# Ten blocks of expert rows instead of eleven, a seventh weight buffer, and a later start for the gathers of stored results

## The chip, the cores and the metric

The kernel runs on one core of one Trainium2 chip. The metric is the device time of one launch in microseconds (us). Three runs of the kernel before gave 803.15, 804.07 and 806.66 us, so the median is 804.07 us.

A core has a matrix engine (TensorE, PE in the profile), a vector engine (DVE), a scalar engine (ACT), GpSimd (POOL) and a sync engine (SP) that here only issues transfers. Sixteen DMA engines serve all queues. PE writes its products to eight banks of PSUM; everything else lies in SBUF or in device memory.

## The reference: what is computed

A trunk of two layers over 384 tokens (128 context, 256 latent) of width 1024, in float32. Each layer has a mixer (attention and a state-space scan behind one input projection, one output projection) and then a mixture of experts. The change concerns the mixture alone:

```python
def moe_ffn(h, w_router, router_bias, w_gate_l, w_up_l, w_down_l):
    ...
    best = jnp.argmax(grp_score, axis=-1)
    masked = jnp.where(in_group, sel, NEG_INF)
    _, idx = lax.top_k(masked, TOP_K)          # TOP_K = 2 of 16 experts
    ...
    hid = jax.nn.silu(einsum('nd,edf->enf', t, w_gate_l)) * einsum('nd,edf->enf', t, w_up_l)
    hid = hid * gates.T[:, :, None]
    out = jnp.einsum('enf,efd->nd', hid, w_down_l)
```

An expert has a gate and an up matrix (1024 x 256) and a down matrix (256 x 1024), 1 MiB each. So a layer reads 48 MiB of expert weights. The 384 tokens make 768 choices. The number of tokens that the reference sends to each expert can be counted from the given inputs. In layer 0, experts 0 to 15 get 38, 35, 30, 51, 43, 30, 42, 31, 99, 72, 105, 52, 45, 13, 45 and 37 tokens. In layer 1 they get 57, 50, 46, 37, 21, 24, 31, 26, 48, 76, 62, 38, 69, 49, 47 and 87.

## The kernel before, in words

**Blocks.** The kernel computes rows of tokens in blocks of 128. The shapes are fixed when the program is built, while the counts are known only when it runs. So each expert has a capacity in rows. In the kernel before, experts 0 and 1 are fixed and have 128 rows each. The other 14 are ranked by their counts at run time: the four most loaded have 128 rows each, the ten others 64. A block holds one expert of 128 rows or two of 64, which makes eleven blocks (`BLOCKS`, `PAIRS`).

**Overflow.** If an expert gets more tokens than its capacity, the rest is computed in extra rounds. DVE takes the largest excess over the capacities (`combination`) and derives `rounds`; each engine then reads that number and, if it is over zero, runs `overflow`: per round a loop over all 16 experts, one after the other (`again` on each engine). Of each expert it makes the list of tokens, gathers 128 rows, loads the three matrices (3 MiB), multiplies, and stores 128 rows. SP loads an expert's matrices only once the expert before it has been multiplied, since one pair of buffers serves all. After the 16 experts, six gathers and six pairs of DVE operations add the results to `x`, one after the other (`gather_results`, `add_results`).

**A block on the engines.** POOL gathers the block's rows from `h_rows` by an indirect DMA. PE transposes them (L2202), multiplies with gate and up (`gate_up`, L2212), transposes the hidden rows (L2219) and multiplies with down (`down`, L2228). DVE and ACT carry the data between these (L1556, L984, L1561, L1567, L991). Eight blocks are stored by ACT to `y_exp` in device memory. The last three (`LATE`) stay in SBUF, and PE adds them by products with a selection matrix (L2272). The order on PE is fixed in the code: while block b waits for its hidden rows, the gate-up product of block b+1 runs.

**Where an expert's rows stand in the array.** A block with one expert is multiplied as 128 columns of the array; one with two experts as two tiles of 64 columns, an instruction for each (`n = P // len(slots)`).

**Weights.** SP loads weights into a ring of `SLOTS` = 6 buffers of 2 MiB. A unit is either the gate and up of one expert or the down matrices of a pair. `MOE_UNITS` gives the order, `EARLIER` the unit whose use frees the buffer. The units of ranked experts can be issued only when DVE has written `order` (L1436, semaphore `s_order`). PE waits for a unit by `landed`.

**The end of a layer.** When all blocks but the last three are stored, POOL issues six gathers from `y_exp` (L714), two for each of three groups of 128 tokens. ACT and DVE weight and add them (L1001, L1544), DVE multiplies with the gate (L1549, L1550), then adds the late blocks (L1656). SP loads the next layer's input projection only when the last of these gathers has landed.

Of the kernel before, what the change touches and what calls it, by code (L numbers as in the profile page):

```python
# [12 lines left out]
P = 128  # L13
DM = 1024
KT = DM // P
# [18 lines left out]
FIXED = 2  # L34
# [6 lines left out]
SLOTS = 6  # L41
# [12 lines left out]
for _l in range(DEPTH):  # L54
# [6 lines left out]
    assert len(ORDER) % SLOTS == 0  # L61
# [3 lines left out]
PAIRS = ("fixed", "light", "heavy", "light", "heavy", "light", "light", "light")  # L65
BLOCKS = [(_p, _part) for _p, _kind in enumerate(PAIRS)
          for _part in (((0, 1),) if _kind == "light" else ((0,), (1,)))]
NB = len(BLOCKS)
HEAVY = 2 * PAIRS.count("heavy")
_heavy, _light = iter(range(HEAVY)), iter(range(HEAVY, RANKED))  # L70
RANK_AT = [None if _kind == "fixed" else tuple(next(_heavy if _kind == "heavy" else _light) for _ in range(2))
           for _kind in PAIRS]
GU_BLOCK = [[b for b, (p, part) in enumerate(BLOCKS) if p == pp and k in part][0]
            for pp in range(len(PAIRS)) for k in range(2)]
# [5 lines left out]
LATE_RANKS = [r for p, part in BLOCKS[STORED:] for r in (RANK_AT[p][k] for k in part)]  # L80
assert all(len(part) == 2 for p, part in BLOCKS[STORED:]) and LATE_RANKS == list(range(RANKED - 2 * LATE, RANKED))
stores_of = lambda i: len(range(i, STORED, 2))
DN_BLOCK = [max(b for b, (p, _part) in enumerate(BLOCKS) if p == pp) for pp in range(len(PAIRS))]
MOE_UNITS = []
for _b in range(NB + 1):
    for _p, _ks in ([(BLOCKS[_b][0], BLOCKS[_b][1])] if _b < NB else []) + ([(BLOCKS[_b - 1][0], (2,))] if _b else []):
        MOE_UNITS += [(_p, _k) for _k in _ks if (_p, _k) not in MOE_UNITS]
# [4 lines left out]
def product_order():  # L92

    last = []
    for l in range(DEPTH):
        before = range(MOE_AT[l - 1] + MOE_U if l else 0, MOE_AT[l])
        last += sorted(before, key=lambda u: (u >= IN_AT[l][1], u == IN_AT[l][0], u))
        for b in range(NB + 1):
            if b < NB:
                last += [MOE_AT[l] + UNIT_AT[BLOCKS[b][0], k] for k in BLOCKS[b][1]]  # L100
            if b and DN_BLOCK[BLOCKS[b - 1][0]] == b - 1:
                last += [MOE_AT[l] + UNIT_AT[BLOCKS[b - 1][0], 2]]
    return last
# [4 lines left out]
SLOT, EARLIER = [], []  # L108
for _u in range(len(ORDER)):
    if _u < SLOTS:  # L110
        SLOT.append(_u)
        EARLIER.append(None)
        continue
    _holder = {s: max(v for v in range(_u) if SLOT[v] == s) for s in range(SLOTS)}
    _s = min(_holder, key=lambda s: RELEASED[_holder[s]])
# [10 lines left out]
def hybrid_step(nc, x_prompt, x_sample, cache_k, cache_v, state_ssm, c, c_ctx, norm1_w, norm2_w,  # L126
# [9 lines left out]
    with ctx:  # L136
# [9 lines left out]
        xn = sb("xn", NT, DM)  # L146
# [5 lines left out]
        xpad = sb("xpad", XM * 512)  # L152
# [136 lines left out]
        y_exp = nc.dram_tensor("y_exp", [STORED * CAP, DM], fp32)  # L289
# [6 lines left out]
        landed = [sem(f"landed{i}") for i in range(SLOTS)]  # L296
        s_rows, s_x, s_small, s_state = sem("rows_landed"), sem("x_landed"), sem("small_landed"), sem("state_landed")
        s_snw, s_fnw = sem("snw_landed"), sem("fnw_landed")
# [58 lines left out]

        def gate_up_of(s):

            return ring[:, s, :].rearrange("p (i k f) -> p k i f", i=2, k=KT)  # L360
# [43 lines left out]
        LISTS = ((0, 1), (1, 2), (2, 7), (7, NB))  # L404
        ROWS_AT = 5
# [36 lines left out]
        def _(sp):  # L442
# [19 lines left out]
            def columns(u, w):  # L462
# [3 lines left out]
                load(u % SLOTS, [(slot(u)[:, 4 * i:4 * i + 4, :], v[:, 4 * i:4 * i + 4, :]) for i in range(2)])  # L466
# [13 lines left out]
            def expert_unit(l, pair, j, u):  # L480

                s = SLOT[u]
                if j < 2:
                    load(u % SLOTS, [(ring[:, s, i * KT * F:(i + 1) * KT * F], by_row(w[l, pair[j]]))
                             for i, w in enumerate((w_gate, w_up))])
                else:
# [1880 lines left out]
```

## Time and profile before

| | us |
|---|---|
| median of 3 runs | 804.07 |
| the profiled execution | 801.22 |
| its span, first to last instruction | 799.5 |
| PE busy | 743.1 (93%) |
| DVE busy | 328.9 (41%) |
| ACT busy | 216.1 (27%) |
| POOL busy | 142.9 (18%) |
| DMA, mean rate | 265 GB/s, 211.56 MB |

All rows that are shown are from the one profiled execution, whose own time is 1.6 us over its span. It is 2.9 us under the median of the three runs. PE is busy nearly all the time, but a busy PE says little by itself: the profile must be read stage by stage. The mixture of experts of layer 0 runs from about 255 to 414 us, that of layer 1 from about 631 to the end.

### The profile page before, as it was taken

Reading aid. Unit: us, or ns where it says so; the run is one execution under the profiler, and the core shown is the slowest. Engines: PE = TensorE matmul, PEld = TensorE weight load, DVE = VectorE, ACT = ScalarE, POOL = GpSimd, SP = SyncE. Lnnn points to the kernel's source line nnn. Section 1 sums busy time; section 2 is a strip of 40 time slices with the busy share of each in tenths; the row PEclk is TensorE's granted clock in tenths of the full one; section 3 lists DMA queues with packets and bytes.
Section 4 is the critical chain, followed back from the end, with each engine's and each line's share of the span. In section 5 each row is a group of like instructions: output and inputs, shape, how many; then the busy total and the mean of one; then the engine's idle time right before and its main releaser. Section 6 shows DMA issues by size and latency. Waiting matters only on the chain. (4 is left out here: it accounts for less than half of the span.)

```text
span 799.5 us, 9607 instructions
## 1 busy us (share of the span) xinstructions
PE 743.1 (93%) x3542; PEld 374.4 (47%) x3542; DVE 328.9 (41%) x870; ACT 216.1 (27%) x491; POOL 142.9 (18%) x238
## 2 busy tenths in 40 slices
PE   3999998999998999999899999888999899999994
PEld 1456653545446444443344755344544654444331
DVE  2023534735536453212272252564643744331136
ACT  2210255734023110111312025493411311101121
POOL 4146041120010200000112404122000120000102
PEclk9999999999999999999999999999999999999998
DMA  8997228899601999999897233345420399999961
GB/s 321 387 342 250 95 106 295 308 362 403 240 0 80 374 392 420 421 424 423 312 389 245 88 105 112 108 170 228 155 105 1 121 420 377 418 425 422 422 241 79
DMA packets 66340, 211.56 MB, mean 265 GB/s; under 512 B 7883, under 2 KB 8755, under 8 KB 54003
## 3 DMA queue, kind: packets, MB, share of 16 engines
q1 hardware_dynamic: 52744, 179.33, 57.9%
q10 hardware_dynamic: 7851, 17.70, 5.8%
q0 software_dynamic: 5696, 13.89, 4.8%
q8 instruction: 29, 0.48, 0.2%
q14 instruction: 20, 0.16, 0.1%
HBM read 202.02 MB, written 13.93 MB: 270 GB/s over the span
## 5 line engine op out<-in xcount | busy, mean ns | idle before, releaser
L2212 PE MATMUL bank<-ring,work 128*64 128x512 f32 (+1 forms) x512 | 156.5, 596 | 4.1 <-DMA ring<-in_w_up_dram 3.2
L2212 PEld LDWEIGHTS bank<-ring,work 128*64 128x64 f32 (+1 forms) x512 | 58.6, 157 | 96.2 <-issue 94.6
L2228 PE MATMUL bank<-ring,xs_tok 128*64 128x512 f32 (+1 forms) x256 | 79.9, 597 | 2.5 <-DVE xs_tok L1567 1.4
L1567 DVE COPY xs_tok<-bank 128x256 f32<-128x256 f32 x22 | 9.3, 425 | 150.7 <-PE bank L2219 150.7
L1850 PE MATMUL bank<-hT,ring 128*128 128x384 f32 x192 | 62.2, 486 | 0.0
L1724 PE MATMUL bank<-ring,cpad 128*32 128x512 f32 x384 | 48.6, 632 | 6.2 <-DMA ring<-in_w_ada_dram 5.4
L1850 PEld LDWEIGHTS bank<-hT,ring 128*128 128x128 f32 x192 | 36.5, 190 | 25.0
L2228 PEld LDWEIGHTS bank<-ring,xs_tok 128*64 128x64 f32 (+1 forms) x256 | 28.3, 157 | 39.6 <-issue 36.9
L984 ACT ACTIVATE xs_tok<-bank 128x256 f32<-128x256 f32 x22 | 8.5, 386 | 138.4 <-PE bank L2212 138.4
L2108 PE MATMUL bank<-ring,xn 128*128 128x512 f32 x96 | 43.6, 597 | 0.0
L991 ACT ACTIVATE qkv<-bank 128x512 f32<-128x512 f32 x40 | 21.7, 595 | 80.0 <-PE bank L2228 80.0
L2108 PE MATMUL bank<-ring,xs_tok 128*128 128x512 f32 x96 | 43.2, 592 | 0.0
L1795 PE MATMUL bank<-ring,hT 128*128 128x512 f32 x96 | 42.8, 597 | 0.4 <-ACT hT L797 0.4
L1907 PE MATMUL bank<-ring,hT 128*128 128x512 f32 x96 | 42.3, 593 | 0.0
L707 POOL DMA_INDIRECT hT<-h_rows,idx x18 | 18.4, 1024 | 124.0 <-PE bank L2202 77.1
L1556 DVE COPY work<-bank 128x512 f32<-128x512 f32 x42 | 27.1, 686 | 10.9 <-PE bank L2202 10.9
L1164 DVE SCALAR_TENSOR_TENSOR conv<-xpad,prm,conv 128x388 f32<-128x388 f32 x48 | 29.9, 623 | 1.7
L2108 PEld LDWEIGHTS bank<-ring,xs_tok 128*128 128x128 f32 x96 | 18.2, 190 | 23.0 <-issue 23.0
L1795 PEld LDWEIGHTS bank<-ring,hT 128*128 128x128 f32 x96 | 17.7, 190 | 22.6 <-issue 20.4
L1907 PEld LDWEIGHTS bank<-ring,hT 128*128 128x128 f32 x96 | 17.8, 190 | 20.1 <-issue 20.1
L2108 PEld LDWEIGHTS bank<-ring,xn 128*128 128x128 f32 x96 | 17.4, 190 | 19.2 <-issue 19.2
L1724 PEld LDWEIGHTS bank<-ring,cpad 128*32 128x32 f32 x384 | 10.8, 113 | 30.0 <-issue 21.7
(389 smaller groups left out, 1062.1 us busy)
## 6 DMA issues: line engine op xcount, KB each, us to landing
ring<-in_w_ada_dram SPq DMA_DIRECT2D x48, 1024.0 KB, 8.9
ring<-in_w_gate_dram SPq DMA_DIRECT2D x32, 1024.0 KB, 8.2
ring<-in_w_up_dram SPq DMA_DIRECT2D x32, 1024.0 KB, 12.3
ring<-in_w_down_dram SPq DMA_DIRECT2D x32, 1024.0 KB, 10.9
ring<-in_w_in_dram SPq DMA_DIRECT2D x16, 1024.0 KB, 14.4
ring<-in_w_out_dram SPq DMA_DIRECT2D x8, 1024.0 KB
y_exp<-qkv ACTq DMA_DIRECT2D x16, 512.0 KB, 8.1
xpad<-gate_rows ACTq DMA_DIRECT2D x6, 512.0 KB, 5.7
```

The costliest lines, as they stand in the source:

```text
L707: pool.indirect_dma_start(out=xg[b % 4], out_offset=None, in_=h_rows[:, :], in_offset=bass.IndirectOffsetOnAxis(ap=idx[:, b:b + 1], axis=0 ...
L991: act.activation(y_buf(e)[:, hf * 512:(hf + 1) * 512], bank[5 + hf][:, :], ACT.Copy).then_inc(s_yc, 1)
L1164: ins = dve.scalar_tensor_tensor(out=conv[:, m, :], in0=xpd[:, m, k:k + CONVW], scalar=tap(k), in1=conv[:, m, :], op0=ALU.mult, op1=ALU.add)
L1556: dve.tensor_copy(xgT[:, b, hf * 512:(hf + 1) * 512], bank[3 + hf][:, :]).then_inc(s_xgc, 1)
L1567: dve.tensor_copy(hidT[:, b, :], bank[2][:, 0:F]).then_inc(s_htc, 1)
L1724: last = mm(bank[ADA_BANK][ADA_TILE * q:ADA_TILE * (q + 1), :], cpad[:, c:c + ADA_TILE], slot(ADA_AT[j])[:, kt, :], start=j == a and kt < ...
L1795: last = mm(bank[t][:, :], tok(kt, t), slot(u[0])[:, kt, :], start=kt == 0, stop=kt == KT - 1)
L1850: last = mm(bank[(6 + m) % 8][:, 0:3 * P], slot(v)[:, kt, col:col + P], hT[:, kt, :], start=kt == 0, stop=kt == KT - 1)
L1907: last = mm(bank[4 + t][:, :], tok(kt, t), slot(u[3])[:, kt, :], start=kt == 0, stop=kt == KT - 1)
L2108: last = mm(bank[2 * t + hf][:, :], mixed[:, t, kt * P:(kt + 1) * P] if kt < 4 else xs_tok[:, t, (kt - 4) * P:(kt - 3) * P], slot(u + hf)[ ...
L2212: last = mm(bank[b][i * n:(i + 1) * n, :].rearrange("p (i f) -> p i f", i=2), rows_T[:, kt * P + i * n:kt * P + (i + 1) * n], gate_up_of(s ...
L2228: last = mm(bank[5 + hf][i * n:(i + 1) * n, :], hidT[:, b, f * P + i * n:f * P + (i + 1) * n], w[:, f, hf * 512:(hf + 1) * 512], start=f = ...
```

## The change

1. **Ten blocks.** Three experts are fixed, with 96 rows each. Of the 13 ranked ones the most loaded has 128 rows, the next three have 96, the other nine 64. The experts that have 96 rows share blocks with parts of 64 and 32 rows. Blocks 0, 2 and 4 hold parts of 64, 32 and 32 rows, one instruction for each; block 3 one of 128 rows; the others two of 64. Seven blocks are stored, three are late.
2. **A seventh buffer.** `extra` is a view of memory that held `xn` and `xpad`, now in one tensor, `arena`. It is free once the rows of `h` are stored, and used until block 5. A unit's semaphore is now one of seven (`LANDED`).
3. **Order of loads.** More is loaded before the ranking is known: experts 0, 1 and 2, and the down matrices of 0, 1 and 2. One unit is split for it (`SPLIT`).
4. **DVE's order.** The list of block 1 (now all fixed experts) is made behind `order`, and its row numbers behind another product.
5. **Gathers of results.** POOL waits for the last weight unit of the layer before it issues the six gathers. ACT and DVE weight them behind the last block.
6. **Capacities** in `combination` follow the new sizes; the overflow code is the same.

```diff
-FIXED = 2
+FIXED = 3
-SLOTS = 6
+SLOTS, EXTRA, LANDED = 6, 6, 7
...
+FULL, WIDE = 1, 4
+FIXED_CAP = 96
+cap_of = lambda r: CAP if r < FULL else HALF + CAP // 4 if r < WIDE else HALF
...
+Q = CAP // 4
+wide = lambda x: ((x, 0, HALF), (x, HALF, Q))
+BLOCKS = [parts_of(*wide(0), (1, 0, Q)),
+          parts_of((1, Q, HALF), (2, 0, HALF)),
+          parts_of(*wide(3), (2, HALF, Q)),
+          parts_of((4, 0, CAP)),
+          parts_of(*wide(5), (6, 0, Q)),
+          parts_of((6, Q, HALF), (7, 0, HALF))] + [parts_of((x, 0, HALF), (x + 1, 0, HALF)) for x in (8, 10, 12, 14)]
...
+SPLIT = (1, 2)
+MOE_UNITS = [(0, 0), (0, 1), (1, 0), (0, 2), SPLIT]
...
-        xn = sb("xn", NT, DM)
+        arena = sb("arena", NT * DM + XM * 512)
+        xn = arena[:, 0:NT * DM].rearrange("p (t c) -> p t c", t=NT)
...
+        xpad = arena[:, NT * DM:]
+        extra = arena[:, DM:DM + UNIT]
...
+                u = MOE_AT[l] + MOE_U - 1
+                pool.wait_ge(landed[u % LANDED], 32 * (u // LANDED + 1))
                 pool.wait_ge(s_yidx, l + 1)
...
                 for e in range(NB):
                     if e + 1 < NB:
                         silu(e + 1, (e + 1) % 2)
-                    if e == NB - 2:
-                        act.wait_ge(s_yidx, l + 1)
-                        weighted(0)
-                    if e == NB - 1:
-                        weighted(1)
-                        weighted(2)
...
                     store(e, e % 2)
+                act.wait_ge(s_yidx, l + 1)
+                for t in range(NT):
+                    weighted(t)
...
+                one_hots(*LISTS[1])
                 step(dve.tensor_tensor(by_rank, rt[:, 1, :, FIXED:E].unsqueeze(2).broadcast_to([P, NT, RANKED, RANKED]),
                                        perm.unsqueeze(1).broadcast_to([P, NT, RANKED, RANKED]), ALU.mult))
+                slot_tokens(1)
...
-                    dve.memset(cap_row[:, 0:FIXED], float(CAP))
+                    dve.memset(cap_row[:, 0:FIXED], float(FIXED_CAP))
...
-                    step(dve.tensor_scalar(cap_row[:, FIXED:E], rank, float(HEAVY), float(HALF), ALU.is_le, ALU.mult))
+                    dve.tensor_scalar(cap_stored[:, FIXED:E], rank, float(FULL), float(Q), ALU.is_le, ALU.mult)
+                    step(dve.tensor_scalar(cap_row[:, FIXED:E], rank, float(WIDE), float(Q), ALU.is_le, ALU.mult))
...
-                    step(dve.tensor_scalar(cap_row[:, FIXED:E], cap_row[:, FIXED:E], float(HALF), None, ALU.add))
+                    step(dve.scalar_tensor_tensor(out=cap_row[:, FIXED:E], in0=cap_row[:, FIXED:E], scalar=float(HALF),
+                                                  in1=cap_stored[:, FIXED:E], op0=ALU.add, op1=ALU.add))
...
                     step(dve.tensor_tensor(count, count, cap_row, ALU.subtract))
                     step(dve.tensor_reduce(top, count, AX.X, ALU.max))
...
-                        for i, s in enumerate(slots):
-                            last = mm(bank[b][i * n:(i + 1) * n, :].rearrange("p (i f) -> p i f", i=2),
-                                      rows_T[:, kt * P + i * n:kt * P + (i + 1) * n], gate_up_of(s)[:, kt, :, :],
+                        for s, at, n in parts:
+                            last = mm(bank[b][at:at + n, :].rearrange("p (i f) -> p i f", i=2),
+                                      rows_T[:, kt * P + at:kt * P + at + n], gate_up_of(s)[:, kt, :, :],
                                       start=kt == 0, stop=kt == KT - 1)
```

The first place is on PE, at the first block of a layer. Before, after the transposes of the rows, block 0 (one expert) is multiplied in instructions of 128 columns (the size is that of the output, columns by stream), four of gate-up ahead of the transposes of the next rows, and later the four of down:

```order
L2202 MATMUL bank<-ident,hT 128x128 x8
...
L2212 MATMUL bank<-ring,work 128x512 x4
L2202 MATMUL bank<-ident,hT 128x128 x8
...
L2219 MATMUL bank<-ident,xs_tok 128x128 x2
L2202 MATMUL bank<-ident,hT 128x128 x8
L2228 MATMUL bank<-ring,xs_tok 128x512 x4
```

Now block 0 alternates between an instruction of 64 columns and two of 32, eight times in gate-up and four times in down:

```order
L2279 MATMUL bank<-ident,hT 128x128 x8
...
L2288 MATMUL bank<-ring,work 64x512
L2288 MATMUL bank<-ring,work 32x512 x2
L2288 MATMUL bank<-ring,work 64x512
L2288 MATMUL bank<-ring,work 32x512 x2
...
L2303 MATMUL bank<-ring,xs_tok 64x512
L2303 MATMUL bank<-ring,xs_tok 32x512 x2
```

The tile size changes twice in each step of 128 input features, which happens nowhere in the kernel before.

On DVE, between the counts and the lists of the ranked blocks, the kernel before makes both fixed lists ahead of `order` (L1436); `idx` is what POOL's gathers wait for:

```order
L1418 TENSOR_TENSOR conv<-slots_f,qT 128x384 x2
...
L1406 SCALAR_TENSOR_TENSOR idx<-qT,bank 128x1
L1431 TENSOR_REDUCE qT<-qT 128x14
L1405 COPY qT<-bank 128x1
L1406 SCALAR_TENSOR_TENSOR idx<-qT,bank 128x1
...
L1436 TENSOR_SCALAR qT<-qT 128x14
L1438 TENSOR_TENSOR xs_tok<-qT 128x588
```

Now the second `idx`, that of block 1, stands behind `order` (L1523) and two more operations:

```order
L1485 SCALAR_TENSOR_TENSOR idx<-qT,bank 128x1
...
L1523 TENSOR_SCALAR qT<-qT 128x13
L1498 TENSOR_TENSOR conv<-slots_f,qT 128x3x64 x2
L1526 TENSOR_TENSOR xs_tok<-qT 128x507
L1484 COPY qT<-bank 128x1
L1485 SCALAR_TENSOR_TENSOR idx<-qT,bank 128x1
```

`order` moved ahead by the two operations of the second list and one of the first two lists, and block 1's row numbers moved behind it.

On SP, ahead of the first expert number that is read (`TENSOR_LOAD`), the kernel before loads two experts and two down matrices, and then three whole units:

```order
L460 DMA ring<-in_w_gate_dram 128x2048
L460 DMA ring<-in_w_up_dram 128x2048
L460 DMA ring<-in_w_down_dram 128x2048 x2
L510 TENSOR_LOAD qT
...
L460 DMA ring<-in_w_gate_dram 128x2048
L460 DMA ring<-in_w_up_dram 128x2048
```

Now three experts and three down matrices stand ahead of it; one unit and a half in the ring and one in `arena` follow:

```order
L527 DMA ring<-in_w_down_dram 128x2048 x3
L576 TENSOR_LOAD qT
...
L527 DMA ring<-in_w_gate_dram 128x2048
L527 DMA ring<-in_w_up_dram 128x2048
L527 DMA ring<-in_w_down_dram 128x2048
...
L527 DMA arena<-in_w_gate_dram 128x2048
L527 DMA arena<-in_w_up_dram 128x2048
```

Three MiB of the layer's 48 are thus asked for earlier than before, and 2 MiB more can be asked for while the ring is full.

## Rows read from the trace of the kernel before

**Rows 1.** Windows: us, busy PE PEld DVE ACT POOL, granted clock, DMA share, GB/s.
```profile
240.00:260.00 20.00, 17.64 (x146) 13.30 (x145) 13.04 (x45) 6.98 (x17) 1.99 (x3) 1.00 0.20 80
340.00:360.00 20.00, 20.00 (x74) 8.26 (x76) 3.66 (x7) 2.56 (x5) 0.00 (x0) 1.00 1.01 422
```
**Rows 2.** Timeline of PE, layer 0: start, us, what [idle before <-releaser].
```profile
268.22 1.04 PE L2202 MATMUL bank<-ident,hT 128*128 128x128 f32 x8
...
293.03 3.60 PE L2228 MATMUL bank<-ring,xs_tok 128*128 128x512 f32 x8
296.46 7.03 PE L2212 MATMUL bank<-ring,work 128*128 128x512 f32 x16
303.33 0.38 PE L2219 MATMUL bank<-ident,xs_tok 128*128 128x128 f32 x2
...
316.16 3.60 PE L2228 MATMUL bank<-ring,xs_tok 128*128 128x512 f32 x8
319.69 7.09 PE L2212 MATMUL bank<-ring,work 128*64 128x512 f32 x32
326.71 0.44 PE L2219 MATMUL bank<-ident,xs_tok 128*128 128x128 f32 x2
...
380.52 7.09 PE L2212 MATMUL bank<-ring,work 128*64 128x512 f32 x32 [1.81 <-DMA ring<-in_w_up_dram]
...
394.47 3.65 PE L2228 MATMUL bank<-ring,xs_tok 128*64 128x512 f32 x16 [1.09 <-DMA ring<-in_w_down_dram]
```
**Rows 3.** Timeline of SP, layer 0.
```profile
260.85 0.36 SPq L460 DMA_DIRECT2D ring<-in_w_gate_dram  x1
261.30 0.38 SPq L460 DMA_DIRECT2D ring<-in_w_up_dram  x1
...
396.48 12.70 SPq L460 DMA_DIRECT2D ring<-in_w_in_dram  x8
```
**Rows 4.** Timeline of POOL, layer 0.
```profile
258.70 1.18 POOL L707 DMA_INDIRECT hT<-h_rows,idx  x1 [12.77 <-DVE idx L1406]
260.19 1.05 POOL L707 DMA_INDIRECT hT<-h_rows,idx  x1 [0.30 <-issue]
...
383.68 0.99 POOL L714 DMA_INDIRECT xn<-y_exp,y_idx  x1 [0.31 <-issue]
```
**Rows 5.** Line L707 by itself: the gathers of rows, its last row.
```profile
DMA to landing us min/median/max: 9.0/10.1/11.7
```
**Rows 6.** Timeline, layer 0: first product of block 0's rows, end of the layer.
```profile
262.76 1.06 PE L2202 MATMUL bank<-ident,hT 128*128 128x128 f32 x8 [1.15 <-DMA hT<-h_rows,idx]
...
396.49 1.15 ACT L1001 ACTIVATE xn<-xn,wt 128x1024 f32<-128x1024 f32 x1 [0.38 <-DMA xn<-y_exp,y_idx]
397.73 1.28 DVE L1544 SCALAR_TENSOR_TENSOR xn<-xpad,wt,xn 128x1024 f32<-128x1024 f32 x1 [0.30 <-ACT xn L1001]
...
403.05 1.29 DVE L1656 TENSOR_TENSOR xn<-bank,xn 128x512 f32<-128x512 f32 x2 [1.52 <-PE bank L2272]
```
**Rows 7.** Timeline, end of layer 1.
```profile
774.26 1.15 ACT L1001 ACTIVATE xn<-xn,wt 128x1024 f32<-128x1024 f32 x1 [2.43 <-DMA xn<-y_exp,y_idx]
...
780.61 1.29 DVE L1656 TENSOR_TENSOR xn<-bank,xn 128x512 f32<-128x512 f32 x2 [1.30 <-issue]
```
**Rows 8.** Windows around a fall of the granted clock; columns as in the first group.
```profile
510.20:514.16 3.96, 1.90 (x10) 0.88 (x10) 3.00 (x12) 3.80 (x18) 2.46 (x4) 1.00 0.69 260
514.16:517.58 3.42, 3.42 (x20) 0.59 (x16) 1.04 (x4) 1.28 (x4) 0.03 (x1) 0.50 0.00 0
```
**Rows 9.** Timeline of PE: tiles of 32 columns, then of 64.
```profile
160.50 1.04 PE L1724 MATMUL bank<-ring,cpad 128*32 128x512 f32 x8
161.47 0.44 PE L1952 MATMUL bank<-qkv,ckv 128*64 128x256 f32 x2
```
**Rows 10.** Timeline, layer 0: hidden rows of a block with nothing beside them.
```profile
387.65 0.38 ACT L984 ACTIVATE xs_tok<-bank 128x256 f32<-128x256 f32 x1 [7.81 <-PE bank L2212]
388.36 0.41 DVE L1561 TENSOR_TENSOR xs_tok<-xs_tok,bank 128x256 f32<-128x256 f32 x1
388.50 3.65 PE L2228 MATMUL bank<-ring,xs_tok 128*64 128x512 f32 x16 [0.52 <-DVE xs_tok L1567]
```

More of the change, by code:

```diff
@@ L60, with parts_of @@
     MOE_AT.append(len(ORDER))
-    assert len(ORDER) % SLOTS == 0
     ORDER += [("moe", MOE_U * _l + j) for j in range(MOE_U)]
-PAIRS = ("fixed", "light", "heavy", "light", "heavy", "light", "light", "light")
-BLOCKS = [(_p, _part) for _p, _kind in enumerate(PAIRS)
-          for _part in (((0, 1),) if _kind == "light" else ((0,), (1,)))]
-NB = len(BLOCKS)
[L69 to L74, printed above, removed]
+FULL, WIDE = 1, 4
+FIXED_CAP = 96
+RANK_OF = [None if _x < FIXED else _r for _x, _r in zip(range(E), (0, 0, 0, 1, 0, *range(2, RANKED)))]
+assert sorted(_r for _r in RANK_OF if _r is not None) == list(range(RANKED))
+cap_of = lambda r: CAP if r < FULL else HALF + CAP // 4 if r < WIDE else HALF
+def parts_of(*parts):
+    at, out = 0, []
+    for x, lo, n in parts:
+        out.append((x, lo, n, at))
+        at += n
+    assert at == CAP
+    return tuple(out)
+Q = CAP // 4
[6 more added lines that the diff above has]
+          parts_of((6, Q, HALF), (7, 0, HALF))] + [parts_of((x, 0, HALF), (x + 1, 0, HALF)) for x in (8, 10, 12, 14)]
+NB = len(BLOCKS)
+experts_of = lambda b: list(dict.fromkeys(x for x, *_ in BLOCKS[b]))
+pairs_of = lambda b: list(dict.fromkeys(x // 2 for x in experts_of(b)))
+for _x in range(E):
+    _cap = FIXED_CAP if RANK_OF[_x] is None else cap_of(RANK_OF[_x])
+    _held = sorted((lo, n) for parts in BLOCKS for x, lo, n, _at in parts if x == _x)
+    assert sum(n for _lo, n in _held) == _cap and all(a + n == b for (a, n), (b, _n) in zip(_held, _held[1:]))
+GU_BLOCK = [max(b for b in range(NB) if x in experts_of(b)) for x in range(E)]
 BUFS, HOTS = 4, 5
@@ L108, with in_extra @@
 SLOT, EARLIER = [], []
+EXTRA_LAST = STORED
+def in_extra(u):
+    for at in MOE_AT:
+        if at + SLOTS <= u < at + MOE_U:
+            p, k = MOE_UNITS[u - at]
+            return (GU_BLOCK[2 * p + k] <= EXTRA_LAST) if k < 2 else DN_BLOCK[p] < EXTRA_LAST
+    return False
 for _u in range(len(ORDER)):
@@ L465, in columns @@
                     sp.wait_ge(*used(EARLIER[u]))
-                load(u % SLOTS, [(slot(u)[:, 4 * i:4 * i + 4, :], v[:, 4 * i:4 * i + 4, :]) for i in range(2)])
+                load(u % LANDED, [(slot(u)[:, 4 * i:4 * i + 4, :], v[:, 4 * i:4 * i + 4, :]) for i in range(2)])
             def ada_unit(u, n):
@@ L2193, in _ @@
                 lists(0)
+                clock_kept(2, 8)
                 lists(1)
[L2195 to L2198 removed]
                 def rows_transposed(buf, done):
@@ L2320, in again @@
                     pe.wait_ge(o_htc, q + 1)
-                    down(0, [ring[:, OVER_DN, 0:2 * DM]], o_dn)
+                    down(0, [(ring[:, OVER_DN, 0:2 * DM], 0, P)], o_dn)
                 def banks_read(steps):
```

206 lines of the change are left out of this document (114 added, 92 removed).

## The prediction

> **What bounds the kernel now.** I first read the windows of 20 us. Before 260 us the DMA engines move 80 GB/s; in the mixture of experts they move 422 GB/s with a busy share of 1.01, and PE is busy for all 20 of 20 us [rows 1]. So both are full there. Then I read PE's timeline. A block costs a down product and a gate-up product, each with small transposes: from the down at 293.03 to the next but one at 316.16, two blocks pass in 23.13 us, or 11.6 us each [rows 2]. PE waits only at the end, 1.81 us for one unit of weights and 1.09 us for the last [rows 2].
>
> How the DMA engines bound the stage follows from bytes. SP issues the first unit of a ranked expert at 260.85 and the next layer's weights at 396.48 [rows 3], 135.6 us later. Between lie 21 units of 2.10 MB and 25 transfers of rows of 0.52 MB (11 gathers of tokens, 8 stores, 6 gathers of results), 57.2 MB in all. That makes 422 GB/s, the rate of the window. The stage is thus bounded by DMA, with PE some 3 us less loaded. At the end DVE takes the last gathered result at 397.73 and reaches the late blocks at 403.05, having waited 1.52 us for PE [rows 4]. In layer 1 the gather is what the chain of waits goes through: ACT waits 2.43 us for it at 774.26 [rows 5].
>
> **The ten-block layout and its capacities.** The largest term is no term of the steady state. The new capacities of the ranked experts are 128 once, 96 three times, then 64. In layer 0 the ranked counts are 105, 99, 72, 52 and fewer: the second expert has 99 tokens and 96 rows. The largest excess is 3, `rounds` is 1, and every engine enters the overflow loop for all 16 experts. The kernel before had 128 rows for 99 tokens and no excess. In layer 1 the counts 87, 76, 69, 62, 49 fit, and so do the fixed experts in both layers (57 at most, of 96).
>
> The trace of before has no overflow, so the price of an expert is built from like operations. The count starts when PE has ended the down product of the expert before.
> - Weights: SP may issue only then. They are 3.15 MB. The gather of this expert's rows and the store of the last one's add 1.05 MB. At 422 GB/s [rows 1] that is 9.9 us; with some 2 us from the issue to the first data, 12 us.
> - Rows: the token list, its row numbers and POOL's issue take some 2 us. Under load a gather lands 9.0 us or more after its issue [rows 6]. Eight transposes (1.06 us, [rows 4]) and the copies (1.3 us) follow: 13.4 us. This ends later than the weights.
> - Gate-up at 128 columns: 6.87 us, from 296.46 to 303.33 [rows 2].
> - Hidden rows: gate-up of the last block ended at 380.52 + 6.87 = 387.39, its product on DVE at 388.77: 1.4 us; transposes and copy of the block before took until 388.50: 1.1 us [rows 2, 7]. Nothing hides these here: 2.5 us.
> - Down: 3.43 us, from 293.03 to 296.46 [rows 2].
> - Clock: after 4 us in which PE was busy for 1.90 us, the granted clock was 0.50, and it came back after 3.4 us in which PE was busy all the time [rows 8]. The two values are 1.2 and 2.4 GHz. In the loop PE is idle for some 12 of 27 us. I take 3.4 us of work at half speed per expert and the transposes at half too, +2.5 us.
> - Branch: reading the number of rounds and the branch cost DVE 1.30 us [rows 5]; of the loop's own branch I take 0.5 us.
>
> The sum is 13.4 + 6.9 + 2.5 + 3.4 + 2.5 + 0.5 = 29.2, and I take 29 us; 16 experts make 464 us. Its lower end is 24 us, if the gather hides behind the weights and the clock stays up (12 + 6.9 + 2.5 + 3.4, less a little overlap). Its upper end is 40 us, if all 12 us of PE's work run at half clock. That is 384 to 640 us for 16. Behind the loop stand six gathers in a row. Each takes 0.9 us from DVE to POOL and 4.1 us alone (258.70 to 262.76) [rows 4, 9]. Two operations of 1024 columns on DVE follow (1.28 us each) [rows 4], so one costs 7.9 us and six cost 47 us. With some 5 us for entering and for the row numbers, the round costs 464 + 52 = 516 us. Nothing hides it: the late results and the next layer need `x` behind it.
>
> **The rest of the change, by bytes.** After `order` there now are 19.5 units instead of 21 and 23 transfers of rows instead of 25: 53.0 MB, or 125.6 us at 422 GB/s. Three things take from these 10 us. The six gathers of results now run alone. They are issued 1.3 us apart, and one alone lands after 4.1 us: 10.6 us instead of 7.5 for the bytes, 3 us lost. Early in the stage the ring is still held by blocks 1 and 2: seven units are in or under way, and 5.2 MB last 12.4 us, while the next unit waits for gate-up of block 0, and the one of block 2 ends about 34 us after `order`. I estimate 5 us of idle DMA there, from 0 to 8. And block 1's row numbers now come behind `order`. POOL issued that gather at 260.19 [rows 9], ahead of SP's first load at 260.85 [rows 3], and PE took its rows at 268.22 without waiting [rows 2]. Now it is issued near 262, behind 3 MB of weights, and lands 9 us later, near 271: PE, and with it the ring, is some 3 us late (0.5 to 4), half of which the idle DMA above already has. What remains is about 2 us by which the last gather lands earlier. Layer 0 gains 1.5 us more, since DVE's wait for PE goes with the eleventh block, and layer 1 gets 2 us. That is -6 us in sum, from -16 (no idle DMA) to +2. The weighting behind the last block costs nothing: its gathers land later than that. The added operations of `combination` (some 0.2 us each) lie beside PE's second block, and the iotas of the start beside the first loads.
>
> A further term is open: blocks 0, 2 and 4 change between a tile of 64 columns and tiles of 32. Tiles of one size run side by side: 32 instructions of 64 columns take 7.02 us (319.69 to 326.71), 16 of 128 take 6.87 us [rows 2]. A change of size costs 0.10 us (316.16 to 319.69 is 3.53, where 293.03 to 296.46 without one is 3.43) and 0.15 us on the way back [rows 2]. From 32 to 64 columns it costs 0.11 us: eight instructions in two groups from 160.50 would let the next start at 161.36, and it started at 161.47 [rows 10]. In all these rows the tiles share columns. If the different sizes run side by side where they do not, the term is 0, which I take. If not, it is the second rival.
>
> On this the Trainium skill, TensorEngine Tiling (Array Packing), Key Properties, says that a change of tiling mode, not just of tile, drains the engine. By that rule the three blocks would be serial, and the sum would be that of the second rival; the rows above agree with a drain where tiles share columns, and none shows tiles that do not.
>
> **The sum.** 801.22 us, the profiled execution's own time, less 6 and plus 516 is 1311 us. The median lies 2.9 us above that execution: 804.07 + 510 = 1314 us.
>
> **Rivals.**
> 1. *The round runs, and the tile sizes do not run side by side.* A step of 128 input features takes 0.86 us now (6.87 / 8). It would take 0.86 for 64 columns, 0.86 for the two tiles of 32 and two changes of 0.25 us together: +1.11 us. Every instruction appears twice in the trace (16 issued, x32 shown). If the two halves alternate there are four changes, +1.36 us. A mixed block has 12 steps, so three blocks cost 40 to 49 us a layer. The block that is gone gives back 11.6, the waits for weights 3, and the later gather takes 3. PE then bounds the stage: +28 to +37 us a layer, 54 to 72 in sum, 60 to 78 over my forecast. That is 1383 us. For it: the change costs in each row where sizes differ. Against it: only shared columns were seen.
> 2. *The round does not run* (the other side). It is decided at one point: whether the second ranked expert of layer 0 has over 96 tokens on the chip. For it: no overflow ran in before, so nothing in the trace shows one. Against it: 99 is three over, and rounding would have to turn three choices. The time would then be 804 - 6 = 798 us, and 863 us with serial tiles.
> 3. *The round is cheap or dear.* With 24 us an expert it is 1230 us; with 40 us it is 1490 us. It decides the ends of the range.
>
> **How the numbers follow.** The round with free mixing of tiles has 0.50, the round with serial tiles 0.40, no round 0.10 (0.05 faster by over 0.5%, 0.02 within, 0.03 slower by serial tiles). A difference of 0.5%, 4 us, is about what a measurement of this kernel can tell. So faster has 0.05, the same 0.02, slower 0.93. The likeliest case gives 1314 us, by itself 1218 (24 us an expert, -12 elsewhere) to 1410 (35 us an expert). The second case sits at 1383. The range reaches from 1215 to 1440; outside it lie the cases with no round and the ends of the dear ones.
>
> **What would show it.** The round: instructions of the overflow loop on all engines between the last block of layer 0 and the late results, 16 times three matrices loaded, HBM reads up by about 50 MB of weights, and a granted clock that falls and comes back with each expert. PE from one down product to the next: 29 us. The mixed blocks: gate-up of block 0 in 7 us, or in 16 to 18. The rest: DMA at 422 GB/s from `order` on, with a gap near the third block, and the gathers of results 1.3 us apart behind the last load. My forecast is wrong if the loop is not there, or if an expert costs under 24 or over 35 us.

## The result: 1430.4 us, and the profile after

| | us |
|---|---|
| before, median of 4 runs | 804.73 (803.15 to 806.66) |
| after, median of 4 runs | 1430.43 (1428.14 to 1430.73) |
| ratio, 95% interval | 1.779 (1.775 to 1.783) |
| forecast | 1314 (1215 to 1440) |

The changed kernel is 626 us slower. Before has a fourth run here, so its median is 804.73 and not 804.07. The forecast, its second case (1383 us) and the top of what the first case was given by itself (1410 us) all lie below; the range holds the result with 10 us to spare. The span of the profiled execution grew from 799.5 to 1429.0 us.

One correction ahead: the prediction numbers some groups of rows otherwise than the section that shows them. Its [rows 4] is Rows 6, its [rows 5] Rows 7, its [rows 6] Rows 5, its [rows 7] Rows 10, its [rows 9] Rows 4 and its [rows 10] Rows 9; 1, 2, 3 and 8 are the same. From here on [rows N] is the group with that number in the section.

The windows of after by stage (busy time of each engine with the number of instructions, then the granted clock, the DMA share and GB/s):

```profile
254.00:321.00 67.00, 63.88 (x272) 20.31 (x271) 24.46 (x104) 5.76 (x11) 8.36 (x8) 1.00 0.61 229
321.00:436.00 115.00, 102.57 (x441) 33.14 (x439) 25.67 (x62) 14.70 (x26) 7.91 (x8) 0.96 0.85 338
436.00:940.00 504.00, 254.73 (x594) 117.77 (x595) 55.05 (x159) 23.49 (x48) 15.02 (x16) 0.71 0.38 144
940.00:1005.00 65.00, 11.79 (x31) 5.46 (x30) 20.51 (x19) 1.15 (x2) 6.70 (x8) 0.62 0.32 120
```

From 436 to 940 us stands a stage that before did not have: the overflow loop, with PE busy for half of it and a mean granted clock of 0.71. In the experts of layer 0 the DMA engines move 229 and 338 GB/s, at shares of 0.61 and 0.85, where they moved 422 at a share of 1.01 [rows 1]. PE is busy for most of both windows. So the DMA engines no longer bound that stage. PE's timeline there answers to [rows 2]:

```profile
290.72 8.01 PE L2303 MATMUL bank<-ring,xs_tok 128*64 128x512 f32 x24
298.66 15.95 PE L2288 MATMUL bank<-ring,work 128*64 128x512 f32 x48
314.54 0.44 PE L2295 MATMUL bank<-ident,xs_tok 128*128 128x128 f32 x2
314.81 1.04 PE L2279 MATMUL bank<-ident,rot 128*128 128x128 f32 x8
315.78 3.65 PE L2303 MATMUL bank<-ring,xs_tok 128*64 128x512 f32 x16
319.36 7.13 PE L2288 MATMUL bank<-arena,work 128*128 128x512 f32 x16
```

The first two rows are down of block 0 and gate-up of block 2, both with parts of 64, 32 and 32 columns (a row gives one shape for all its instructions, and shows each twice). From the start of one row to the next it is 7.94 us for 4 steps and 15.88 for 8, or 1.99 us a step. Blocks 1 and 3, which follow, have equal parts or one: 3.58 and 6.97 us, as before. The last down product of layer 0 starts at 420.44 and ends at 424.1; before it started at 394.47 and ended at 398.1 [rows 2]. That is 26 us.

Then the round. One iteration of its loop, all engines but the weight loads of PE:

```profile
507.91 0.22 PE L2260 MATMUL bank<-tok_id,conv 128*128 128x2 bf16 x3
508.25 0.33 SPq L602 DMA_DIRECT2D ring<-in_w_gate_dram  x1
509.15 0.38 SPq L604 DMA_DIRECT2D ring<-in_w_down_dram  x1
509.49 0.94 POOL L801 DMA_INDIRECT hT<-h_rows,idx  x1 [29.92 <-DVE idx L1694]
520.04 1.97 PE L2279 MATMUL bank<-ident,hT 128*128 128x128 f32 x8 [11.91 <-DMA hT<-h_rows,idx]
522.65 0.68 DVE L1697 COPY hT<-bank 128x512 f32<-128x512 f32 x1
523.46 9.76 PE L2288 MATMUL bank<-ring,hT 128*128 128x512 f32 x16 [1.46 <-DVE hT L1697]
533.26 0.38 ACT L1104 ACTIVATE xs_tok<-bank 128x256 f32<-128x256 f32 x1 [24.07 <-PE bank L2288]
535.11 3.70 PE L2303 MATMUL bank<-ring,xs_tok 128*128 128x512 f32 x8 [0.52 <-DVE xs_tok L1702]
538.65 0.22 PE L2260 MATMUL bank<-tok_id,conv 128*128 128x2 bf16 x3
```

From one list product to the next it is 30.74 us. The rows land 10.55 us after their issue, and that ends PE's wait. The first expert takes longer, 40.67 us, since its weights stand in the queue behind 8 MB of the next layer's projection, which SP issued at 428.55:

```profile
445.06 1.97 PE L2279 MATMUL bank<-ident,hT 128*128 128x128 f32 x8 [8.46 <-DMA hT<-h_rows,idx]
461.66 9.95 PE L2288 MATMUL bank<-ring,hT 128*128 128x512 f32 x16 [14.63 <-DMA ring<-in_w_down_dram]
477.03 0.22 PE L2260 MATMUL bank<-tok_id,conv 128*128 128x2 bf16 x3
```

Behind the loop come the last store, six gathers one after the other, and the late blocks:

```profile
938.25 1.08 ACT L1107 ACTIVATE hT<-bank 128x512 f32<-128x512 f32 x2 [5.20 <-PE bank L2303]
939.50 0.34 ACTq L1110 DMA_DIRECT2D y_over<-hT  x1
949.21 1.00 POOL L793 DMA_INDIRECT hT<-y_over,qT  x1 [39.35 <-issue]
955.13 1.28 DVE L1719 SCALAR_TENSOR_TENSOR hT<-hT,qT,arena 128x1024 f32<-128x1024 f32 x1 [17.76 <-DMA hT<-y_over,qT]
995.41 1.22 DVE L1722 TENSOR_TENSOR x<-x,hT 128x1024 f32<-128x1024 f32 x1
997.33 1.29 DVE L1735 TENSOR_TENSOR arena<-bank,arena 128x512 f32<-128x512 f32 x2 [0.70 <-DVE x L1722]
```

DVE reaches the late blocks at 997.33, against 403.05 before [rows 6]. So of 629.5 us of span 26 are in the experts of layer 0 and 568 between their last down product and this row. Of the 35 that are left, 34 come with the experts of layer 1: their routing begins 595.5 us later than before (1226.53 for 631.01), the end 629.5 us later.

### The profile page after: what moved, and what is told of

Same layout as the page of the kernel before. It is cut to its first block and busy times, and to the rows that moved or that the text cites. A ratio compares the mean times of both kernels' runs of the same rounds, so it can differ in the third digit from the quotient of the medians.

```text
span 1429.0 us, 12151 instructions
## 1 busy us (share of the span) xinstructions
PE 1055.4 (74%) x4388; PEld 475.5 (33%) x4388; DVE 394.8 (28%) x1049; ACT 236.2 (17%) x533; POOL 160.1 (11%) x255
## 5 line engine op out<-in xcount | busy, mean ns | idle before, releaser
L2279 PE MATMUL bank<-ident,hT 128*128 128x128 f32 x256 | 48.2, 350 | 192.2 <-DMA hT<-h_rows,idx 192.2
L2288 PE MATMUL bank<-ring,work 128*64 128x512 f32 (+1 forms) x640 | 182.2, 604 | 0.8 <-DVE work L1636 0.8
L2288 PE MATMUL bank<-ring,hT 128*128 128x512 f32 x256 | 155.4, 775 | 36.5 <-DVE hT L1697 21.9
L2303 PE MATMUL bank<-ring,xs_tok 128*64 128x512 f32 (+2 forms) x480 | 158.3, 603 | 9.3 <-DVE xs_tok L1702 8.3
L2279 PEld LDWEIGHTS bank<-ident,hT 128*128 128x128 f32 x256 | 39.4, 182 | 195.4 <-DMA hT<-h_rows,idx 189.4
L2288 PEld LDWEIGHTS bank<-ring,hT 128*128 128x128 f32 x256 | 62.6, 252 | 122.5 <-issue 107.4
L2288 PEld LDWEIGHTS bank<-ring,work 128*64 128x64 f32 (+1 forms) x640 | 42.9, 128 | 124.2 <-issue 122.4
L2303 PEld LDWEIGHTS bank<-ring,xs_tok 128*64 128x64 f32 (+2 forms) x480 | 47.1, 146 | 97.8 <-issue 82.6
L1845 PE MATMUL bank<-ident,arena 128*128 128x128 f32 x96 | 14.0, 299 | 54.1 <-DVE arena L1191 54.1
L2187 PE MATMUL bank<-ring,arena 128*128 128x512 f32 x96 | 43.6, 597 | 0.0
L1874 PE MATMUL bank<-ring,hT 128*128 128x512 f32 x96 | 42.8, 597 | 0.4 <-ACT hT L878 0.4
L1986 PE MATMUL bank<-ring,hT 128*128 128x512 f32 x96 | 42.3, 593 | 0.0
```

The source lines that it names most:

```text
L1845: last = tr(bank[norm_bank(k, t)[hf]][:, j * P:(j + 1) * P], xn[:, t, kt * P:(kt + 1) * P], ident[:, :])
L1874: last = mm(bank[t][:, :], tok(kt, t), slot(u[0])[:, kt, :], start=kt == 0, stop=kt == KT - 1)
L1986: last = mm(bank[4 + t][:, :], tok(kt, t), slot(u[3])[:, kt, :], start=kt == 0, stop=kt == KT - 1)
L2187: last = mm(bank[2 * t + hf][:, :], mixed[:, t, kt * P:(kt + 1) * P] if kt < 4 else xs_tok[:, t, (kt - 4) * P:(kt - 3) * P], slot(u + hf)[ ...
L2279: last = tr(bank[3 + kt // 4][:, kt % 4 * P:(kt % 4 + 1) * P], buf[:, kt * P:(kt + 1) * P], ident[:, :])
L2288: last = mm(bank[b][at:at + n, :].rearrange("p (i f) -> p i f", i=2), rows_T[:, kt * P + at:kt * P + at + n], gate_up_of(s)[:, kt, :, :], ...
```

## The experiments

The theory was: a round of some 568 us, and tiles of different size that do not run side by side. The rivals were other causes for each. All ratios are to the kernel before, run on the same chip.

**no_round.**

```diff
-step(dve.tensor_scalar(R(4)[:, 9:10], top, 0.0, None, ALU.is_gt))
+step(dve.tensor_scalar(R(4)[:, 9:10], top, 8.0, None, ALU.is_gt))
```

> The kernel after, but the number of overflow rounds is counted from an excess of over 8 tokens and not of over 0, so the round is not run. What it leaves out: the second ranked expert's contribution to its last 3 tokens in layer 0. In the trace of the kernel after the late results are added 594.3 us later than in before (997.33 against 403.05); 26 us of that are there already at the last down product of layer 0 (424.1 against 398.1). Theory: the round costs 568 us and nothing else comes from it, so the time is 1430 - 568 = 862 us (855 to 870), 58 us over before, 26 us of it in layer 0's experts and 34 in layer 1's. Rival: the longer stage of layer 1 is an effect of the round (later loads, another clock); then layer 1 goes back to its length before, and the time is near 830 us.

Measured: 867.95 us, ratio 1.078 (1.072 to 1.084). The round costs 562.5 us. The rest stays 64 us over before. The first row of the next layer's projection, in before and then in no_round:

```profile
414.18 5.31 PE L1795 MATMUL bank<-ring,hT 128*128 128x512 f32 x12
```

```profile
448.62 5.31 PE L1874 MATMUL bank<-ring,hT 128*128 128x512 f32 x12
```

It starts 34.4 us later, and the span is 67.0 us longer, so layer 1 has 32.6 us of its own. The rival, a slowness of layer 1 that comes from the round, is out.

**before_round.** The kernel before with an excess of its own:

```diff
-step(dve.tensor_scalar(cap_row[:, FIXED:E], rank, float(HEAVY), float(HALF), ALU.is_le, ALU.mult))
+step(dve.tensor_scalar(cap_row[:, FIXED:E], rank, float(HEAVY), float(HALF // 2), ALU.is_le, ALU.mult))
```

> The kernel before, with 96 instead of 128 rows counted for each of the four heavy ranked experts in the capacities: the last 3 tokens of the second ranked expert of layer 0, and 9 of the first, go through an overflow round. Nothing is left out. It prices the round without the other edits. Theory: the same 568 us as read in after, so 804 + 568 = 1372 us (1360 to 1384). Rival, the sum of the forecast: 516 us, 1320 us. If the late start of the result gathers or the new buffers add to the round in after, this one is under 1360.

Measured: 1369.14 us, ratio 1.701 (1.692 to 1.710), or 565 us for the round. It costs the same in both kernels, so neither the new buffers nor the later gathers add to it. My 516 is too low by 46 to 49 us.

**tiles32.** For a block with three parts (`gate_up` and `down` both take `same_size(parts)`):

```diff
+def same_size(parts):
+    if len(parts) < 3:
+        return parts
+    return [(s, at + i, Q) for s, at, n in parts for i in range(0, n, Q)]
```

> As the kernel without the round, and blocks 0, 2 and 4 are multiplied in four instructions of 32 columns where there were one of 64 and two of 32. Theory: tiles of different size wait for each other, tiles of one size run side by side. Then a step of 128 input features takes 0.86 us again where the trace of after shows 1.99, the three blocks lose 12 steps x 1.13 = 13.5 us each, 81 us for six, as far as the DMA engines allow: PE is no longer what bounds, and the time is what I forecast for the rest of the change, 798 us (790 to 806). Rival: the cost comes from having more than two column tiles or three different weights in a step, or from the 32-column form itself. Then four instructions a step cost as much or more, 862 us or over (up to 880).

Measured: 808.23 us, ratio 1.0046 (1.0016 to 1.0076), 59.7 us under no_round. PE's rows for the same two products as above:

```profile
288.20 3.64 PE L2309 MATMUL bank<-ring,xs_tok 128*32 128x512 f32 x32
291.65 7.05 PE L2294 MATMUL bank<-ring,work 128*32 128x512 f32 x64
```

Four instructions of 32 columns take 0.86 us a step, as long as one of 128. The rival fell: neither the number of column tiles nor of different weights matters, nor the 32-column form. The time is 10 us over my 798 and outside its 790 to 806; early_gather and early_weight look for these 10 us.

**grouped.**

```diff
+groups = [[q for q in parts if q[2] == n] for n in sorted({q[2] for q in parts}, reverse=True)]
+for g, kt in [(g, kt) for g in range(len(groups)) for kt in range(KT)]:
```

> As the kernel without the round, but in blocks 0, 2 and 4 the instructions of 64 columns all come first and those of 32 behind them: one change of size in a product, not two in each step. Theory: two costs, each its own: sizes do not overlap (0.86 us a step becomes 1.72) and each change costs about 0.12 us. Grouping takes only the second away: 12 steps x 0.25 us = 3 us a block, 18 us in sum, gate-up of a mixed block 13.9 us instead of 15.9, and the time is 862 - 18 = 844 us (838 to 850). Rival: the change itself is the whole cost (a drain of over 1 us for a pair of changes) and alone a tile of 64 or a pair of 32 would be quick; then grouping gives back nearly all of it, and the time is near 800 us. A third: no cost per change at all, 862 us.

Measured: 855.55 us, ratio 1.063 (1.058 to 1.069), 12.4 us under no_round.

```profile
290.71 7.21 PE L2305 MATMUL bank<-ring,xs_tok 128*64 128x512 f32 x24
297.84 14.07 PE L2289 MATMUL bank<-ring,work 128*64 128x512 f32 x48
```

Gate-up now takes 14.01 us to its next row, twice the 6.98 of one size. This order leaves only the two tiles of 32 to run side by side, so it does not by itself test whether the sizes could overlap. It gives the time of one size after the other, 1.75 us a step, and the alternating order takes longer still, 1.99 us: there nothing overlaps. Alternating, a gate-up product changes size 15 times, grouped once. So the 1.87 us that went (15.88 less 14.01) belonged to 14 changes, 0.13 us each; in down 6 changes fewer give 0.81 us (7.13 for 7.94), again 0.13 each. A block gives 2.7 us, and six give 16; the spans differ by 15.3 us, the medians by 12.4. I had expected 18 and 844 us (838 to 850), counted from 862 us; the kernel it was built from measured 868. Both rivals fell: grouping gives back neither nearly all nor nothing.

**early_gather and six_buffers**, each from tiles32. early_gather looks for the 10 us:

```diff
-u = MOE_AT[l] + MOE_U - 1
-pool.wait_ge(landed[u % LANDED], 32 * (u // LANDED + 1))
```

> As tiles32 (four tiles of 32 columns in the mixed blocks, no overflow round), but POOL does not wait for the last weight unit before it issues the six gathers of stored results. tiles32 took 808.2 us where I had forecast 798. In its trace the last down product of layer 0 ends 0.4 us earlier than in before (397.65 plus 3.65 for 398.05 plus the same), yet the next layer's first projection starts at 420.57 and not at 414.18, and the six gathers begin only at 389.41. Theory: the late start of the gathers costs the 6.4 us in layer 0 and some 3 us at the end, and taking the wait away gives them back: 799 us (796 to 803). Rival: the DMA engines are full, and 3.1 MB of gathers among the weights push the last weights back by 7.5 us, so that it comes to the same, 808 us (805 to 812).

(397.65 and 398.05 are already the ends of the two products; the 3.65 is not to be added.) Measured: 809.09 us, ratio 1.0068 (1.0041 to 1.0095), no difference from tiles32 that can be told. But the rival's reason is not what the trace shows either: the last down product ended 1.2 us earlier than in tiles32, not later. ACT and DVE still took the gathered rows behind the last block:

```profile
371.57 0.99 POOL L793 DMA_INDIRECT rot<-y_exp,y_idx  x1 [47.66 <-DMA y_exp<-qkv]
397.49 3.22 ACT L1081 ACTIVATE arena<-arena,wt 128x1024 f32<-128x1024 f32 x3
398.67 1.29 DVE L1622 SCALAR_TENSOR_TENSOR arena<-rot,wt,arena 128x1024 f32<-128x1024 f32 x1 [6.24 <-ACT arena L1081]
419.10 5.31 PE L1872 MATMUL bank<-ring,hT 128*128 128x512 f32 x12
```

six_buffers sets `in_extra` to return False.

> As tiles32, but no unit is placed in the seventh buffer. Theory: the seventh buffer lets SP load 2.1 MB at 263 us, while PE still holds the ring; without it this load waits for gate-up of block 0, the DMA engines idle for up to its 5 us, in each layer: 808.2 + 10 = 818 us (812 to 822). Rival: the ring is not what limits the stage after block 2, and the time is the same, 808 us (806 to 811).

Measured: 819.99 us, ratio 1.0194 (1.0167 to 1.0221), 12 us over tiles32, for 10 expected. The seventh buffer is worth what the theory says. (The section on the change has it used until block 5; the trace of after shows it in the gate-up of block 6 too, from 372.50 us.) From 270 to 280 us, first tiles32, then six_buffers:

```profile
270.00:280.00 10.00, 8.38 (x56) 3.67 (x58) 3.70 (x13) 0.38 (x1) 4.04 (x4) 0.66 0.73 276
```

```profile
270.00:280.00 10.00, 7.36 (x56) 2.77 (x58) 3.96 (x13) 0.38 (x1) 3.91 (x4) 0.83 0.38 115
```

Over the 50 us from 260 to 310 the DMA share is 0.87 in tiles32 and 0.77 in six_buffers, which is 5 us of idle more, as the theory has it for a layer.

**early_weight.** As early_gather, with the weighting where before had it:

```diff
                    silu(e + 1, (e + 1) % 2)
+               if e == NB - 2:
+                   act.wait_ge(s_yidx, l + 1)
+                   weighted(0)
+               if e == NB - 1:
+                   weighted(1)
+                   weighted(2)
...
-               act.wait_ge(s_yidx, l + 1)
-               for t in range(NT):
-                   weighted(t)
...
-               weighted(0)
+               if e == NB - 2:
+                   weighted(0)
```

> As early_gather, and in addition ACT and DVE weight the gathered results where the kernel before did, the first group while the last block but one is in hand, the others with the last block. early_gather took 809.1 us, as tiles32: its gathers were issued at 371.57 and not at 389.41, but its weighting began only at 397.49, behind the last block, and layer 1's first projection started 22.7 us after the end of the last down product (396.4 to 419.1), where before takes 16.1 us (398.05 to 414.18). Theory: not the gathers but the place of the weighting is what costs, 6.6 us in layer 0 and some 3 us at the end: 809.1 - 9.6 = 799.5 us (796 to 803). Rival: ACT and DVE then wait for gathers in the middle of the last blocks and hold up PE's hidden rows by as much, 808 us (805 to 811).

Measured: 797.18 us, ratio 0.9914 (0.9885 to 0.9942), 12 us under early_gather. This is the missing piece:

```profile
389.51 1.28 DVE L1625 SCALAR_TENSOR_TENSOR arena<-rot,wt,arena 128x1024 f32<-128x1024 f32 x1 [0.34 <-ACT arena L1081]
394.76 2.60 DVE L1625 SCALAR_TENSOR_TENSOR arena<-arena,wt 128x1024 f32<-128x1024 f32 x2 [1.30 <-ACT arena L1081]
413.10 5.31 PE L1876 MATMUL bank<-ring,hT 128*128 128x512 f32 x12
```

DVE is through with weighting at 397.36 and not at 402.60, though the last down product ended 1 us later, and the next layer starts 6.0 us earlier. The weighting in its early place with the gathers still late was not run. In tiles32 the last gather is issued at 395.89, and ACT, late as it is, still waits 0.36 us for the last rows at 401.27; here DVE is through at 397.36. So the early place alone could not have given all of it.

**clean_late, clean_early, clean_order, clean_best.** Ten blocks without parts of 32, and without a round for these counts:

```diff
+FIXED = 4
+FULL, WIDE = 4, 4
+FIXED_CAP = 64
...
+BLOCKS = [parts for x in range(0, E, 2)
+          for parts in ((parts_of((x, 0, CAP)), parts_of((x + 1, 0, CAP))) if x in (4, 8) else
+                        (parts_of((x, 0, HALF), (x + 1, 0, HALF)),))]
```

> Ten blocks with tiles of 128 and 64 columns alone, and nothing left out: four fixed experts with 64 rows each in blocks 0 and 1, four ranked ones with 128, eight with 64. These capacities hold all tokens of both layers (57 at most in the fixed experts, fifth ranked 52 and 62), so no round is run. The seventh buffer and the late gathers stay. All six units of the fixed experts are loaded before the ranking, 18 behind it. Theory: 1.5 units less than tiles32 after the ranking, 3.1 MB or 7.5 us a layer at 422 GB/s: 808 - 15 = 793 us (786 to 800). Rival: with six buffers held by the fixed experts only one unit can be loaded until gate-up of block 0 is done, the DMA engines idle for 7 us more, and nothing is won: 808 us (803 to 812).

> As clean_late, without POOL's wait for the last weight unit before the gathers of results. Theory: as in early_gather the wait costs 4 to 9 us over the two layers, so it is 4 to 9 us below clean_late, 786 us (780 to 792). Rival: within 2 us of clean_late.

> As clean_early (tiles of 128 and 64 columns alone, no round needed, nothing left out), and the weighting stands where the kernel before had it, as in early_weight. Theory: the same 6 to 10 us, 794.0 - 9 = 785 us (782 to 789). Rival: no gain, 793 us (791 to 796).

> As clean_order, and DVE makes the list and the row numbers of block 1 ahead of the ranking again, as the kernel before did. In the trace of clean_late PE waits 0.92 us for the second gather at 270.7, in tiles32 3.34 us. Theory: the ring is freed 0.9 us sooner in each layer, 1 to 2 us below clean_order, 784 us (780 to 788). Rival: the products ahead of the ranking delay the first ranked load by as much, no difference that can be measured.

clean_best also moves the list product of block 1 on PE ahead of eight of its filler products. Measured: 792.94 us for clean_late (ratio 0.986, 0.984 to 0.989), 793.96 for clean_early (0.987, 0.984 to 0.989), 779.78 for clean_order (0.970, 0.967 to 0.972) and 781.66 for clean_best (0.972, 0.970 to 0.975). clean_late met its theory. Taking POOL's wait away alone did nothing again, where 4 to 9 us were expected. With the weighting ahead as well the two layers gain 14 us, more than the expected 6 to 10. The place of block 1's list makes no difference that can be measured. clean_order beats both kernels, 3.0% under before:

```profile
300.00:360.00 60.00, 60.00 (x241) 26.36 (x241) 15.34 (x45) 7.48 (x16) 1.97 (x2) 1.00 1.01 421
404.17 5.31 PE L1870 MATMUL bank<-ring,hT 128*128 128x512 f32 x12
```

DMA and PE are both full, as in before, and the next layer starts 10.0 us earlier than there (404.17 for 414.18). It counts on the given inputs: a fixed expert with over 64 tokens, or a fifth ranked one with over 64, would call for a round.

**round_clock**, from before_round, in the loop of PE:

```diff
 slot_tokens(0, 0, o_idm)
+clock_kept(2, 22)
 pe.wait_ge(o_g, 16 * q + 16)
```

> As before_round (1369.1 us), with 22 products of 128 x 256 on a spare bank, 0.45 us each, issued in every iteration of the overflow loop while PE waits for the gathered rows. In the trace of before_round that wait is 11.9 us; behind it the eight transposes take 1.97 us instead of 1.04 and gate-up 9.21 us instead of 6.87, at a granted clock of half. Theory: the clock falls because PE idles, and is kept up by the products: 0.9 + 2.3 = 3.2 us an expert, 16 x 3.2 = 52 us, 1317 us (1308 to 1326). Rival: the clock stays low whatever PE does there, or the wait grows by what the products take, 1369 us or more.

Measured: 1353.37 us, ratio 1.682 (1.678 to 1.686), 15.8 us under before_round. That is 1.0 us an expert, not 3.2. The windows of one iteration, the filler first:

```profile
506.60:516.30 9.70, 9.70 (x48) 8.27 (x46) 0.47 (x3) 1.08 (x2) 0.94 (x1) 1.00 0.86 312
516.40:518.60 2.20, 0.00 (x0) 0.00 (x0) 0.00 (x0) 0.00 (x0) 0.00 (x0) 1.00 1.02 428
518.60:521.40 2.80, 1.33 (x8) 0.94 (x9) 1.29 (x2) 0.00 (x0) 0.00 (x0) 0.63 0.16 67
521.40:524.00 2.60, 2.60 (x3) 1.17 (x4) 0.00 (x0) 0.00 (x0) 0.00 (x0) 0.50 0.00 0
524.00:526.00 2.00, 2.00 (x4) 0.85 (x3) 0.00 (x0) 0.00 (x0) 0.00 (x0) 0.50 0.00 0
526.00:528.00 2.00, 2.00 (x6) 0.92 (x5) 0.00 (x0) 0.00 (x0) 0.00 (x0) 0.96 0.00 0
```

Neither range holds the result: the theory's 1308 to 1326 us is missed by 27 us, the rival's 1369 by 16. The filler keeps the clock at 1.00 while it runs, but PE is then idle for 2.3 us and again for 1.5 us around the transposes. The clock falls to 0.50 (1.2 GHz) all the same, and gate-up pays for it. What a filler through those gaps too would give was not tried.

## Why the prediction was right in its main cause and short by 116 us

The direction and nine tenths of the change come from the term that the forecast put first, the round. Its likeliest case was still not what happened. That case had the round with tiles side by side and was given 1218 to 1410 us; what ran was the second case, the round with serial tiles, at a higher price than its 1383 us. The range holds the result because it was drawn over both cases. (The 1218 is a slip: 24 us an expert and -12 elsewhere give 1228.)

The 116 us between 1314 and 1430 are three terms of the sum: the round 46 us (562.5 for 516), the mixed tiles 60 us (taken as 0), the rest of the change 10 us (+4.1, tiles32 over before, for -6).

- **The round runs** for three tokens over 96: right, and the term that made the sign. Rival 2 is out.
- **Price of an expert**: 30.74 us for 29.2. Up to gate-up it is 15.55 us for 13.4. Of this the landing of the rows is 10.55 for my 9.0. I had taken the least value of the line; its median is 10.1 [rows 5]. And the transposes at half clock, which I had put under the clock, are 0.9. Gate-up, 6.87 plus most of the 2.5 for the clock, is 9.80. The hidden rows take 1.85 for 2.5, down 3.54 for 3.4, and the branch that I gave 0.5 us does not show. For the 2 us from the issue of the weights to the first data I had no row. In the iteration in which SP issues at 538.99 the DMA share is 0.03 from 539 to 540 us and 0.84 in the next microsecond, so it is about 1 us; it is not on the path, since the gate matrix lands 5.1 us and the up matrix 9.5 us after its issue. Against the 29 that I took, 15 experts give 15 x 1.74 = 26 us.
- **The first expert**: 40.67 us, 12 more than my 29. The forecast let all 16 cost the same and forgot what stood in SP's queue ahead of the first load.
- **Behind the loop**: from 938.2 to 996.6 are 58.4 us, for 47. The six gathers with their sums take 47.4 of it, as worked out (7.9 each). The other 11 are the last store, which must land before the first gather; I had left it out of the chain. For entering I had 5 us; 562.5 less 501.8 for the loop and 58.4 leave 2.3. So 26 + 12 + 11 - 3 = 46 us.
- **The mixed tiles**: this step failed. I took the term as 0, with 0.50 against 0.40, because no row showed tiles on different columns. The rival's number was close: 1.99 us a step where it had 0.86 + 1.11 = 1.97, and 26 us in layer 0 at the last down product where it had 28. Every row that I had with a change of size showed a cost [rows 2, 9]; for free mixing there was none, and I still took the open term at its lower end. The Trainium skill, TensorEngine Tiling (Array Packing), Key Properties, says that a change of mode drains the engine. The traces agree: in after 64 and 32 columns are serial even on different columns (1.99 us a step, 0.86 in tiles32), and by grouped each change costs 0.13 us.
- **The other edits, by bytes**: -6 was forecast, +4.1 measured. The idle DMA early in the stage was there: in tiles32 the shares from 260 to 310 us leave 6 us idle against 2 before, for my estimate of 5. What was wrong here is the sentence that the weighting behind the last block costs nothing. Restoring the order of gathers and weighting as a whole gives 11 us over two layers (808.23 to 797.18), where I had 3 us a layer. Early gathers with late weighting give nothing (809.09); the other half alone was not run. early_weight then stands at -6.7 us against before. That this is near my -6 is luck: its gathers are not late, so by my own terms it should stand at -12.
- **DVE's order, the iotas, `combination`**: right as far as seen. PE waits 3.34 us for block 1's gather in tiles32, inside my 0.5 to 4, and not at all in after, where the longer product of block 0 covers it. clean_order and clean_best do not price those 3.34 us: there PE waits 1.34 and 1.10 us with the list behind and ahead of the ranking.

One term was missing from the sum. In tiles32 PE waits 4.21 us for the last gate and up matrices of layer 0, where it waited 1.81 us [rows 2], and the product behind the wait takes 9.49 us to its next row instead of 7.02:

```profile
378.74 9.55 PE L2294 MATMUL bank<-ring,work 128*64 128x512 f32 x32 [4.21 <-DMA ring<-in_w_up_dram]
```

The granted clock is 0.50 from 378.7 to 381.0 and 0.54 from there to 384.0. Layer 1 has the same at 761.73 (8.79 us behind a wait of 4.19).

## What to carry to other kernels

Check a capacity against the counts of the real inputs before anything else: three tokens over a limit cost 562 us, more than everything else in the change together. Keep the column tiles of a product at one size, since four tiles of 32 cost what one of 128 does (0.86 us a step), while one of 64 alternating with two of 32 costs 2.3 times that. When a transfer's result is taken later, follow the engines that use it: asking for the rows early gave nothing as long as ACT and DVE took them late, and 12 us once they took them early too.

## What the runs showed of the hardware that was not expected

- Tiles of 64 and of 32 columns on different columns of the array did not overlap at all: 15.88 us in turn (after), 14.01 with all of one size first (grouped), and 7.0 us in four tiles of 32 (tiles32).
- A clock held at 1.00 by filler fell within a stretch of 5.0 us (516.4 to 521.4) in which PE was busy for 1.33 us, and was 0.50 until about 526 although gate-up ran without a gap from 521.4 on (round_clock).
- One wait of PE of 4.2 us for weights, between products that run at 1.00, was followed by a clock of 0.50 and cost 2.5 us of slower work besides the wait (tiles32, 374.5 to 388.2 us).
